# Gate and up projection of a hybrid decoder layer: the low parts of all weight blocks on VectorE, none on GpSimd

## What is computed

```python
def _conv_glu(h, w_gate, w_up, ffn_conv_w, ffn_conv_b, w_down):
    gate = _causal_dwconv(h @ w_gate, ffn_conv_w) + ffn_conv_b   # width 3
    return (jax.nn.silu(gate) * (h @ w_up)) @ w_down
```

## Time and profile before

| | us |
|---|---|
| median of 3 runs | 3377.02 |
| lowest, highest | 3367.23, 3378.37 |
| the profiled execution's own time | 3377.97 |
| its span, first to last instruction | 3376.3 |
| mean granted TensorE clock over the span | 0.926 |

### The profile page before, as it was taken

One profiled execution on the slowest core, in us unless ns is written; L12 is line 12 of the kernel. 1 busy time (PEld: TensorE's weight loads), 2 busy tenths in 40 slices (PEclk: granted clock), 3 DMA queues, 4 the chain that ended last, 5 costly groups with the idle time before them and its releaser, 6 DMA issues. The chain is left out here.

```text
span 3376.3 us, 49284 instructions
## 1 busy us (share of the span) xinstructions
PE 2882.2 (85%) x18863; PEld 2491.0 (74%) x18863; DVE 1965.1 (58%) x2927; ACT 1186.6 (35%) x2193; POOL 1159.4 (34%) x1242
## 2 busy tenths in 40 slices
PE   6995648997599979999299579888899999699999
PEld 6994538997488868888287467777778888487787
DVE  2214632343255567776589398888897777434444
ACT  3224531221254445554243143332243333323312
POOL 1112430000677600000345245555566666370000
PEclk9997779998699989999699789998999999899999
DMA  5543445222444232220356532322253333696454
GB/s 179 168 133 107 114 139 216 85 74 66 95 103 97 59 92 71 64 63 20 130 177 220 176 100 90 91 88 84 82 174 111 106 94 103 211 335 206 159 163 153
DMA packets 372676, 421.84 MB, mean 125 GB/s; under 512 B 43130, under 2 KB 285318, under 8 KB 371430
## 3 DMA queue, kind: packets, MB, share of 16 engines
q1 hardware_dynamic: 323286, 276.24, 27.1%
q0 software_dynamic: 19168, 70.99, 6.9%
q10 hardware_dynamic: 30000, 71.58, 6.5%
HBM read 258.18 MB, written 160.55 MB: 124 GB/s over the span
## 5 line engine op out<-in xcount | busy, mean ns | idle before, releaser
L2736 PE MATMUL fu_pM<-fu_us_hi,fu_w_hi 128*128 128x512 f32 x1232 | 494.0, 401 | 12.3 <-DVE fu_us_lo L2548 12.1
L2736 PE MATMUL fu_pM<-fu_us_lo,fu_w_hi 128*128 128x512 f32 x1232 | 491.1, 399 | 0.0
L2736 PE MATMUL fu_pM<-fu_us_hi,fu_w_lo 128*128 128x512 f32 x1232 | 489.7, 397 | 0.0
L2736 PEld LDWEIGHTS fu_pM<-fu_us_hi,fu_w_hi 128*128 128x128 f32 x1232 | 238.8, 194 | 65.8 <-DVE fu_us_lo L2548 15.4
L3011 PE MATMUL fd_pM<-fd_bs_hi,fd_a_hi 128*128 128x512 f32 x616 | 245.5, 399 | 42.1 <-DVE fd_bs_lo L2943 26.8
L2736 PEld LDWEIGHTS fu_pM<-fu_us_hi,fu_w_lo 128*128 128x128 f32 x1232 | 238.4, 193 | 51.3
L2736 PEld LDWEIGHTS fu_pM<-fu_us_lo,fu_w_hi 128*128 128x128 f32 x1232 | 238.5, 194 | 49.8
L3011 PE MATMUL fd_pM<-fd_bs_hi,fd_a_lo 128*128 128x512 f32 x616 | 243.6, 395 | 0.0
L3011 PE MATMUL fd_pM<-fd_bs_lo,fd_a_hi 128*128 128x512 f32 x616 | 243.0, 394 | 0.0
L2938 DVE TENSOR_TENSOR fd_a_lo<-fd_a_lo,fd_a_hi 128x1408 fp32r<-128x1408 f32 x56 | 97.0, 1732 | 231.1 <-ACT fd_a_hi L2894 231.1
L2463 ACT ACTIVATE fu_w_hi<-fu_sw 128x512 fp32r<-128x512 f32 x176 | 110.9, 631 | 321.2 <-PE fu_pM L2736 255.9
(11 more groups left out here) (401 smaller groups left out, 7322.4 us busy)
## 6 DMA issues: line engine op xcount, KB each, us to landing
fd_a_lo<-scr_gs ACTq DMA_DIRECT2D x56, 704.0 KB, 4.7
fu_w_raw<-in_w_gate SPq DMA_DIRECT2D x22, 1024.0 KB, 5.8
fu_w_raw<-in_w_up SPq DMA_DIRECT2D x22, 1024.0 KB, 5.3
scr_gs<-fu_sg SPq DMA_DIRECT2D x88, 256.0 KB, 3.6
scr_gs<-fu_acc SPq DMA_DIRECT2D x66, 256.0 KB, 2.9
fd_wd<-in_w_down POOLq DMA_DIRECT2D x11, 1024.0 KB, 9.5
scr_td<-fd_td SPq DMA_DIRECT2D x44, 256.0 KB, 5.6
fd_b_raw<-scr_td SPq DMA_DIRECT2D x44, 256.0 KB, 4.1
```

The lines of the kernel that those rows point to most:

```text
L2736: p = pe.matmul(bank(2 * n + m, i)[:, :], a[:, k, :], x[:, k, :], start=(k == 0 and n_pass == 0), stop=(k == HALVES_K - 1 and n_pass == 2))
```

## The change

`POOL_SPLITS`, its semaphore `w_ready_pool` and GpSimd's `split` go. VectorE makes the low parts of all seven units, in the order of its steps, and everything that waited for either engine's low parts waits for `w_ready` alone. The arithmetic is the same, instruction for instruction; 88 subtractions of 128 x 512 change engine.

```diff
-        POOL_SPLITS = (5, 6)
-        FIRST_SPLITS = UNITS_7 - len(POOL_SPLITS)
...
-        w_ready_pool = r.sem("w_ready_pool")
...
             def load_w(n, m):
                 if n:
-                    sp.wait_ge(w_ready, FIRST_SPLITS * (2 * n + m - 1))
-                    sp.wait_ge(w_ready_pool, len(POOL_SPLITS) * (2 * n + m - 1))
+                    sp.wait_ge(w_ready, UNITS_7 * (2 * n + m - 1))
...
             def weights(n, m):
...
                 if ph:
-                    pool.wait_ge(w_ready, FIRST_SPLITS * ph)
-                    pool.wait_ge(w_ready_pool, len(POOL_SPLITS) * ph)
+                    pool.wait_ge(w_ready, UNITS_7 * ph)
...
-            def split(ph, i):
-                q = UNITS_7 * ph + i
-                pool.wait_ge(w_half, q + 1)
-                pool.tensor_tensor(w_lo[q % RING][:, :, :], operand(ph % 2, i), f(w_hi[q % RING][:, :, :]),
-                                   ALU.subtract).then_inc(w_ready_pool, 1)
-
             for n in range(SETS):
                 weights(n, 0)
-                for i in POOL_SPLITS:
-                    split(2 * n, i)
                 weights(n, 1)
                 if n:
                     products(n - 1)
-                for i in POOL_SPLITS:
-                    split(2 * n + 1, i)
             products(SETS - 1)
...
             def split(q):
                 ph, i = divmod(q, UNITS_7)
-                if i in POOL_SPLITS:
-                    return
                 dve.wait_ge(w_half, q + 1)
...
-                if i in POOL_SPLITS:
-                    pe.wait_ge(w_ready_pool, len(POOL_SPLITS) * (2 * n + m) + POOL_SPLITS.index(i) + 1)
-                else:
-                    pe.wait_ge(w_ready, FIRST_SPLITS * (2 * n + m) + i + 1)
+                pe.wait_ge(w_ready, q + 1)
```

## The result

| | before | changed |
|---|---|---|
| median, us (20 runs each) | 3368.10 | 3376.96 |
| lowest to highest | 3358.51 to 3378.42 | 3371.61 to 3386.02 |
| ratio, 95% interval | | 1.0027 (1.0017 to 1.0037) |

The changed kernel is 8.9 us slower: the same by the 0.3% set in the forecast, close to its edge, and slower by the interval. Forecast was plus 6, range minus 6 to plus 19 around the median known then. That median, 3377.02, was of three runs and lay 9 us above the one of twenty, so it is the difference that was forecast well; the absolute 3383 is 6 us above what was measured.

The account below looks back on a forecast made before the run. In the first half VectorE and TensorE bound the kernel through the halo sums; in the second, TensorE. Ten sets plus 10, first set minus 1, reload minus 3 gave plus 6 us: 3383 against the median, range 3371 to 3396.

Parts of the forecast that it names:

- The loop: First half: TensorE waits about 4.3 us per set for VectorE's halo sums, and VectorE then waits for TensorE's next unit.
- The walk of the set: One first-half set followed row by row: halo sums start 1.5 us later, shorten by 0.5, TensorE resumes 1.0 us later.
- Stretch: VectorE's run of halo sums in a first-half set, 18.0 us; forecast to shorten by 0.5 us.
- The nine holds of before: VectorE instructions under the halo sums ending late beside nine GpSimd instructions: seven full at 1.05 us, two some 0.45 each.
- The clock: TensorE's granted clock after its longer idle time in the first half: no change taken, plus or minus 0.6 us per set.
- the price of a microsecond on VectorE: First half, between the end of the halo sums' predecessor L2605 and the sums' end: one microsecond there is one of the kernel.
- First set and reload: First set with halo sums: minus 1 us; reload of activations between the halves: minus 3 us (bounds minus 5 to plus 1).
- The relief doesn't come: Slower rival, halo sums: eight GpSimd instructions hold up as much as nine, plus 11 us or more, 3388 to 3394; chance 0.33.
- surcharge for the clock: Part of the slower rival: every restart of TensorE at the dear end of the clock, 6 us more.
- The exclusive lock: VectorE and GpSimd exclude each other for a whole instruction; by it alone each removed GpSimd instruction returns up to one hold.
- The rival of the lock: Faster rival: two full holds go from each set's halo sums, minus 0.6 us per set, 3367 in all; chance 0.10.
- the second half's slack: VectorE's 8.3 us of waits per second-half set, said to cover 2.4 to 6.8 us of added work: cost 0.

Follow-up runs that it names:

- filled waits: Unused matmuls ahead of the halo products keep TensorE busy while it waits, 20 in the kernel before, 24 in the changed one: 0.9909 and 0.9934.

## Why the prediction was right, point by point

- *The loop.* Right: the loss is in the first half's sets, and only there. The second half hid all 44 subtractions, as costed.
- *The walk of the set.* Right, nearly row by row. Sums' start: forecast 1.5 later, measured 1.45, by the mechanism named, since the low part of 2236.25 waits for ScalarE's copy. Stretch: forecast 18.0 to 17.5, measured 17.6. The nine holds of before are seven full and two short and the eight after it seven full and one short, as walked. Sum forecast 1.0, measured 1.02 in the means of VectorE's part, 1.08 with the clock taken out by the filled waits. Even the waypoint in the middle fits: L2565, L2582 before, starts 14.5 us after TensorE begins the up phase, where it was 14.2 and the walk had 14.6.
- *The clock.* The term that was mis-sized. I took no change, within 0.6 per set either way; it was plus 0.4, 3.7 us over ten sets, and 0.8 in the first set. It explains why the stage lost 11.8 us and not about 7. The sign that the prediction named for it, the first half's granted clock moving by more than 0.02, was too coarse: from 2000 to 2400 us it is 0.92 in both. So the price of a microsecond on VectorE, one microsecond of the kernel, is a little too low as well: VectorE's part grew by 1.0 us per set, the set by 1.4. That the time still came within 3 us of the forecast has some luck in it: the clock's 4.5 us in the stage were not in the sum, and the measured difference of the medians, 8.9, happens to lie 3 below the stage's 11.8.
- *First set and reload.* The sums of the first set end 0.9 us earlier, as forecast (minus 1), but there too the clock took it back: from their end to the up phase it is 7.05 us and not 6.27. Reload: minus 3 forecast, minus 2.6 measured (88.1 to 85.5 us from the eleventh to the thirteenth L2605), with three holds fewer where I had walked two and a product.
- *The rivals.* "The relief doesn't come" was wrong in its mechanism; its surcharge for the clock was right in kind. That VectorE's occupancy alone decides is refuted for the second half (80% busy and no loss), and in the first half it is where on VectorE the work stands. The rule of the Trainium skill that the prediction named (Perfetto Trace Analysis, Identifying the Most-Contended Engine) is not refuted with it: it picks the engine with the highest occupancy, judging TensorE by its weight loads, and in the second half these are busy 248.51 of 300 us, more than VectorE's 241.12. The exclusive lock of the Trainium skill (SBUF — State Buffer, Who interferes with whom) agrees with the held rows and with 0.90 us per GpSimd instruction taken away, but doesn't say by itself what a removed one gives back: the same removal shortened the stretch by 0.4 us here and by 1.0 with the halo products behind unit 6. The prediction's wording, that instructions reading two SBUF tiles are held, is too narrow: the held L2550 reads one tile and a column of `head`.
- *Slips that changed nothing.* 3377.97 + 6 is 3384.0, not 3384.2. The rival of the lock is the second in the list, not the third. And without the second half's slack a set would have paid 2.4 to 6.8 us by the prediction's own costs, not up to 2.4.

One reason that I gave was too simple. I costed the four subtractions as a sum. They are not one: gate's unit 6 alone costs what all four cost, and so do the other three without it; VectorE's part alone says the same, with 1.0 us per set for all four and for gate's unit 6, and 1.15 for the other three. Their prices overlap because the sums' start and GpSimd's run under them are both tied to the same copy of ScalarE.

## What to carry to other kernels

When work moves between two engines that hold each other up, find the event that pins each of them (here ScalarE's copy, paced by TensorE) and lay the rows of both out from there: work added behind a pinned event cost in full here, work added ahead of it, where it still ended before the event, cost nothing, and the holds depended on how the rows interleave. A bound engine's wait in every loop is better attacked than shifted: delaying GpSimd's four uninvolved instructions and keeping TensorE at work was worth 44 us, five times what the change lost.

## What was not expected

A wait of 4.3 us in a loop of 46 costs TensorE more than itself: with the wait filled and still there, ten sets were 27.8 us shorter. And the loops drift to a common length: the changed kernel's sets begin at 48.29 us and from the fifth on are 47.79 to a hundredth, and the kernels with only gate's unit 6 or with all but it on VectorE end at the same 47.8, though VectorE's part in them differs by 0.15. The stretch from the sums' end to the up phase, where the lower clock lies, makes up for it: 6.9 us in the first, 6.7 in the second. The two kernels with filled waits keep sets of 43.6 and 44.7, a difference equal to VectorE's part. What sets the common length the runs don't show.
